# Six of eight quads in the seven-product form, with two weight sums of each made by accumulating transfers

## The chip, the cores and the metric

The kernel runs on one core of one Trainium2 chip. The metric is the time of one execution on the device in microseconds (us), given as the median of several runs.

## What is computed

A decoder trunk of two layers over 256 tokens of width 2048, in float32. Each layer adds a mixer (attention of two kinds in layer 0, latent attention in layer 1) and then a squared-ReLU MLP, which is where the change lies:

```python
def squared_relu_mlp(h, w_up, w_down):
    a = jnp.square(jax.nn.relu(h @ w_up))       # [256, 2048] @ [2048, 8192]
    return a @ w_down                           # [256, 8192] @ [8192, 2048]
x = x + squared_relu_mlp(rmsnorm(x, ln_mlp_g[layer]), w_up, w_down)
```

## The kernel before

**Number form.** A float32 matrix is handled as two rounded parts, hi (ScalarE, L707) and lo (VectorE, L1009: the value minus hi). A product is three matmuls (hi·hi, hi·lo, lo·hi) of 128x128 against 128x512 or 256 columns.

**Blocks.** The 8192 hidden columns are taken in four blocks (`b0`) per layer, so there are eight MLP blocks. A block has a stage "up" (32 weight pieces, which make the block's activations `a`, 16 tiles of 128), and a stage "down" over four column chunks of 512 of the output. Chunk 0 goes first (8 pieces, 32 to 39), chunks 1 and 2 go together as eight quads (pieces from 40 on, `quad_at(q)`), and chunk 3 goes last (8 pieces).

**Quads.** Quad q takes two k tiles (2q, 2q+1), both token halves and both column chunks: a 2 by 2 product of blocks. A plain quad makes the eight block products: two pieces and 24 matmuls. A fast quad makes seven (Winograd's variant of Strassen's form): 21 matmuls in pieces of 6, 6, 6 and 3, on the raw weights b11 and b21, the sums t0 and t1 ("t13"), the sums t2 and t3 ("t24"), and b22. It needs four sums of weights (`weight_sums`, VectorE, into `t_sum`, two buffers in turn) and four sums of token tiles (`token_sums` on VectorE, `token_sums_hi` on ScalarE L956, `token_sums_lo` on VectorE L1347). Before the change, quads 0, 1, 3, 5 and 7 are fast. Seven PSUM banks X1 to X7 hold the products and X8 the plain quads' last; after the quads ScalarE copies X1 and X8 to `c_sum` (L980), which frees the banks that chunk 3 uses, and VectorE's `combine` puts the products together in steps placed among the following pieces.

**Order of work.** Every engine has one queue in an order written out by hand. A weight is loaded by SyncE in 1 MB loads into four slots of `raw` (two pieces per load in the straight stages; in the quads two loads serve two quads) as soon as lo of the last piece of the load four before is done (`free_slot`). ScalarE makes hi of piece n once TensorE has used piece n-4 (four slots of `halves`), VectorE makes lo of it, TensorE uses it. In iteration j of the down loop, ScalarE and VectorE first split piece j+4 (`AHEAD`), and then do what the tables hang on that j: for VectorE

```python
sums = {35: 0, 37: 1, quad_at(2) - 3: 2, quad_at(4) - 3: 3, quad_at(6) - 3: 4}
```

so the weight sums of fast quad number m stand ahead of that quad's first splits. GpSimd makes constants, some products for the attention, and nothing in the MLP; no transfer is issued by it.

Of the kernel before, what the change touches and what calls it, by code (L numbers as in the profile page):

```python
# [31 lines left out]
P = 128  # L32
# [101 lines left out]
def all_pieces():  # L134
    out, seen = {}, set()

    def put(n, kind, load, half, count=0):
        out[n] = (kind, load, half, kind in ("raw", "b22") and load not in seen, count)
        if kind in ("raw", "b22"):
            seen.add(load)  # L140
    for n in range(P_MIX0, P_MLP0):
        put(n, "raw", n // 2, n % 2)
    for n in range(P_MIX1, P_MLP1):
        put(n, "raw", L_MIX1 + (n - P_MIX1) // 2, n % 2)
    for layer in range(2):
        for b0 in range(NB):
            for i, (kind, load, half) in enumerate(block_plan(layer, b0)):
                count = 15 * block_no(layer, b0) + 3 * load + (1 if kind == "t13" else 3) if kind[0] == "t" else 0
                put(block_base(layer, b0) + i, kind, load, half, count)
    return out  # L150
# [166 lines left out]
def build(nc, x, positions, ln_mix_g, ln_mlp_g, sf_w_in, sf_b_f, fox_q_g, fox_k_g, sf_w_o,  # L317
# [4 lines left out]
    with ExitStack() as ctx:  # L322
# [21 lines left out]
        with nc.sbuf_tensor("sd_last", [P, 4, 2, P], F32R) as sd_last:  # L344
# [63 lines left out]
        t_sum = [mix[:, 4096:6144].rearrange("p (i n) -> p i n", i=4),  # L408
                 heads_flat[:, 0:2048].rearrange("p (i n) -> p i n", i=4)]
        a_sum = heads_flat[:, 2048:2560].rearrange("p (i t) -> p i t", i=4)  # L410
        c_sum = mix[:, 6144:8192].rearrange("p (i n) -> p i n", i=4)

        def sd_of(i):
            return sd[:, i] if i < 4 else sd_last[:]

# [58 lines left out]
        rk_ready, k_scaled = sem("rk_ready"), sem("k_scaled")  # L474
        act_step, dve_step = sem("act_step"), sem("dve_step")
        t_step, a_step, sd_hi, sd_ready = sem("t_step"), sem("a_step"), sem("sd_hi"), sem("sd_ready")
        joint_copied, combined = sem("joint_copied"), sem("combined")
# [11 lines left out]
        def raw_piece(n):  # L489
# [5 lines left out]
            if kind[0] == "t":  # L495
                pair = 0 if kind == "t13" else 2
                return t_sum[load % 2][:, pair:pair + 2].rearrange("p i n -> p (i n)")
            piece = raw[:, load % SLOTS, half * size:(half + 1) * size]
# [108 lines left out]
        def _(pool):  # L607
# [74 lines left out]
            for n in (28, 29):  # L682
                split_out(n)


        @block.scalar
        def _(act):
# [8 lines left out]
            def split_hi(n):  # L696
# [257 lines left out]
            def token_sums_hi(no, i):  # L954
                act.wait_ge(a_step, 20 * no + 4 * i + 4)
# [39 lines left out]
        def _(dve):  # L995
# [317 lines left out]
            def weight_sums(layer, b0, m):  # L1313

                q = FAST_QUADS[m]
                one, two = pair_loads(layer, b0, q // 2)
                done = 15 * block_no(layer, b0) + 3 * m
# [3 lines left out]
                t = t_sum[m % 2]  # L1321
                b11_b12 = raw[:, one % SLOTS:two % SLOTS + 1:two % SLOTS - one % SLOTS, at:at + N]
                b12_b22 = raw[:, two % SLOTS, at:at + 2 * N].rearrange("p (i n) -> p i n", i=2)
                b21 = raw[:, one % SLOTS, at + N:at + 2 * N]
                v.tensor_tensor(t[:, 0:2], b12_b22, b11_b12, ALU.subtract).then_inc(t_step, 1)
                dve.wait_ge(t_step, done + 1)
                v.tensor_tensor(t[:, 2], b12_b22[:, 1], t[:, 0], ALU.subtract).then_inc(t_step, 1)
                dve.wait_ge(t_step, done + 2)
                v.tensor_tensor(t[:, 3], b21, t[:, 2], ALU.subtract).then_inc(t_step, 1)

            def token_sums(no, i):

                done = 20 * no + 4 * i
# [4 lines left out]
                v.tensor_tensor(a_sum[:, 0], y21, y22, ALU.add).then_inc(a_step, 1)  # L1338
                v.tensor_tensor(a_sum[:, 2], y11, y21, ALU.subtract).then_inc(a_step, 1)
                dve.wait_ge(a_step, done + 1)  # L1340
                v.tensor_tensor(a_sum[:, 1], a_sum[:, 0], y11, ALU.subtract).then_inc(a_step, 1)
                dve.wait_ge(a_step, done + 3)
                v.tensor_tensor(a_sum[:, 3], y12, a_sum[:, 1], ALU.subtract).then_inc(a_step, 1)

            def token_sums_lo(no, i):
                dve.wait_ge(sd_hi, 5 * no + i + 1)
                v.tensor_tensor(sd_of(i)[:, :, 1], a_sum, sd_of(i)[:, :, 0].bitcast(F32), ALU.subtract)                 .then_inc(sd_ready, 1)  # L1347
# [5 lines left out]
            def combine(no, step, base):  # L1353
# [5 lines left out]
                if step == 1:  # L1359
                    dve.wait_ge(joint_copied, 2 * no + 2)  # L1360
                    dve.wait_ge(pieces_used, base + quad_at(7) + 3)
                    v.tensor_tensor(p1_p6, X6, p1_p2, ALU.add).then_inc(combined, 1)
                elif step == 2:
# [11 lines left out]
                elif step == 7:  # L1375
                    after(5)
                    v.tensor_tensor(p1_p6_p7, X4, p1_p6_p7, ALU.add).then_inc(combined, 1)
                elif step == 8:
# [14 lines left out]
            def mlp_block(layer, b0):  # L1393
# [3 lines left out]
                for c in range(4):  # L1397
# [29 lines left out]
                for j in range(32, BLOCK_PIECES):  # L1427
# [36 lines left out]
        def _(pe):  # L1464
# [345 lines left out]
            def mlp_block(layer, b0):  # L1810
# [21 lines left out]
                for c in (0, 3):  # L1832
# [3 lines left out]
                    else:  # L1836
                        pe.wait_ge(cols_read, up0 + 4)
                        for q in range(8):
                            if q in FAST_QUADS:
                                pe.wait_ge(sd_ready, 5 * no + FAST_QUADS.index(q) + 1)  # L1840
                                fast_quad(base + quad_at(q), q, added0 + 1)
# [53 lines left out]
```

## Time and profile before

| | |
|---|---|
| median of 3 runs | 2073.39 us (2072.93 to 2074.01) |
| profiled execution | 2073.62 us, of which 2071.9 us from the first to the last instruction |
| TensorE / VectorE / ScalarE / GpSimd busy | 99% / 70% / 52% / 4% |
| memory traffic | 381.96 MB, 184 GB/s on average |
| one MLP block | 172.85 us (four in each layer) |
| eight quads of a block | 40.12 us |

The profile is of one execution. A busy TensorE is one with matmuls in its pipe, not one at its peak. The start-to-start distance of two matmuls, not the duration of one, says how fast it goes.

### The profile page before, as it was taken

The numbers are of one execution on the slowest core, as the hardware profiler recorded it, in microseconds if no ns is written. First come the engines' busy times: TensorE is split into PE (matmuls) and PEld (weight loads), VectorE is DVE, ScalarE is ACT, GpSimd is POOL, SyncE is SP. The second block draws the span as 40 slices with busy tenths as digits, with TensorE's granted clock in tenths as the row PEclk, the third lists the DMA queues.
The fourth block names the chain that finished last, engine by engine and source line by source line (L and its number), as shares of the span: only waits on it lengthen the run. The fifth ranks groups of instructions, "written<-read, shape, count | busy, mean of one in ns | idle before, by whom it ended". The sixth has DMA issues, their size and how long they took to land.

```text
span 2071.9 us, 25827 instructions
## 1 busy us (share of the span) xinstructions
PE 2060.6 (99%) x10360; PEld 1747.0 (84%) x10360; DVE 1453.8 (70%) x1904; ACT 1087.3 (52%) x1554; POOL 80.3 (4%) x120
## 2 busy tenths in 40 slices
PE   8999999999999999999999999999999999999999
PEld 7888888888888888888888898888888888888887
DVE  6545555567966876886797688557886696697787
ACT  6546565454544544554456676444554454454454
POOL 0000000000000000000000255000000000000000
PEclk9999999999999999999999999999999999999999
DMA  8544554555565565565555433465565665656554
GB/s 283 175 155 163 163 164 161 183 183 195 194 195 195 184 215 183 183 223 183 191 195 179 155 126 123 163 188 179 181 225 182 203 203 185 201 183 207 181 183 163
DMA packets 198479, 381.96 MB, mean 184 GB/s; under 512 B 10892, under 2 KB 17112, under 8 KB 198360
## 3 DMA queue, kind: packets, MB, share of 16 engines
q1 hardware_dynamic: 198312, 380.29, 56.4%
q8 instruction: 83, 1.36, 0.3%
q14 instruction: 36, 0.29, 0.0%
q10 hardware_dynamic: 48, 0.02, 0.0%
HBM read 378.19 MB, written 2.10 MB: 184 GB/s over the span
## 4 chain that ended last, share of the span: by engine, by line
PE 99%; POOL 0%; ACT 0%; DVE 0%; DMA 0%; issue 0%; SPq 0%; DVEq 0%; ACTq 0%
PE psum L1547 23%; PE psum L1478 14%; PE psum L1480 14%; PE psum L1479 14%; PE psum L1550 11%; PE psum L1778 5%; PE psum L1777 5%; PE psum L1776 5%; PE psum L1621 1%; PE psum L1704 1%; PE psum L1565 1%; PE psum L1681 0%; PE psum L1520 0%; PE psum L1665 0%; PE psum L1666 0%; PE psum L1705 0%
## 5 line engine op out<-in xcount | busy, mean ns | idle before, releaser
L1009 DVE TENSOR_TENSOR halves<-raw,halves 128x1024 fp32r<-128x1024 f32 (+1 forms) x724 | 854.7, 1189 | 456.4 <-ACT halves L707 451.3
L707 ACT CAST halves<-raw 128x1024 fp32r<-128x1024 f32 (+1 forms) x724 | 730.0, 1019 | 644.0 <-PE psum L1480 341.9
L1547 PE MATMUL psum<-h,halves 128*128 128x512 f32 x2048 | 639.0, 395 | 0.0
L1550 PEld LDWEIGHTS psum<-h,halves 128*128 128x128 f32 x2048 | 380.1, 188 | 87.7
L1550 PE MATMUL psum<-h,halves 128*128 128x256 f32 x2048 | 398.0, 278 | 0.0
L1478 PE MATMUL psum<-halves,a 128*128 128x512 f32 x828 | 325.5, 393 | 0.0
L1480 PE MATMUL psum<-halves,a 128*128 128x512 f32 x828 | 322.6, 390 | 0.0
L1479 PE MATMUL psum<-halves,a 128*128 128x512 f32 x828 | 322.3, 389 | 0.0
L1547 PEld LDWEIGHTS psum<-h,halves 128*128 128x128 f32 x2048 | 314.3, 189 | 2.8
L1478 PE MATMUL psum<-halves,h 128*128 128x512 f32 (+1 forms) x508 | 201.4, 397 | 0.0
L1480 PE MATMUL psum<-halves,h 128*128 128x512 f32 (+1 forms) x508 | 194.9, 384 | 0.0
L1479 PE MATMUL psum<-halves,h 128*128 128x512 f32 (+1 forms) x508 | 194.4, 383 | 0.0
L1480 PEld LDWEIGHTS psum<-halves,a 128*128 128x128 f32 x828 | 155.4, 188 | 32.8
L1478 PEld LDWEIGHTS psum<-halves,a 128*128 128x128 f32 x828 | 155.5, 188 | 31.8 <-ACT nat L774 0.4
L1479 PEld LDWEIGHTS psum<-halves,a 128*128 128x128 f32 x828 | 155.5, 188 | 31.5
L1776 PE MATMUL psum<-halves,a 128*128 128x512 f32 x312 | 121.4, 389 | 0.0
L1777 PE MATMUL psum<-halves,a 128*128 128x512 f32 x312 | 121.4, 389 | 0.0
L1778 PE MATMUL psum<-halves,a 128*128 128x512 f32 x312 | 121.4, 389 | 0.0
L1480 PEld LDWEIGHTS psum<-halves,h 128*128 128x128 f32 x508 | 95.3, 188 | 18.0
L1479 PEld LDWEIGHTS psum<-halves,h 128*128 128x128 f32 x508 | 95.6, 188 | 16.2
L1478 PEld LDWEIGHTS psum<-halves,h 128*128 128x128 f32 x508 | 95.6, 188 | 16.2
L707 ACT CAST halves<-mix 128x1024 fp32r<-128x1024 f32 x48 | 50.6, 1054 | 50.9 <-PE psum L1480 26.7
(251 smaller groups left out, 1861.5 us busy)
## 6 DMA issues: line engine op xcount, KB each, us to landing
raw<-in_mlp_w_up SPq DMA_DIRECT2D x128, 1024.0 KB, 5.3
raw<-in_mlp_w_down SPq DMA_DIRECT2D x128, 1024.0 KB, 5.2
raw<-in_sf_w_in SPq DMA_DIRECT2D x45, 1024.0 KB, 5.0
raw<-in_sf_w_o SPq DMA_DIRECT2D x16, 1024.0 KB, 5.1
raw<-in_mla_w_o SPq DMA_DIRECT2D x16, 1024.0 KB, 5.1
raw<-in_mla_w_down SPq DMA_DIRECT2D x8, 1024.0 KB, 5.1
raw<-in_mla_w_ukv SPq DMA_DIRECT2D x8, 1024.0 KB, 5.5
raw<-in_mla_w_uq SPq DMA_DIRECT2D x8, 768.0 KB, 4.6
```

The lines of the kernel that those rows point to most:

```text
L707: nc.scalar.copy(half_piece(n, 0), raw_piece(n)).then_inc(hi_done, 1)
L1009: v.tensor_tensor(half_piece(n, 1), raw_piece(n), half_piece(n, 0).bitcast(F32), ALU.subtract)\
L1478: mm(bank, x_hi, hi[:, i], start=(k == 0), stop=False)
L1479: mm(bank, x_hi, lo[:, i], start=False, stop=False)
L1480: last = mm(bank, x_lo, hi[:, i], start=False, stop=(k == total_kts - 1))
L1547: last = mm(bank, half_piece(n, 0)[:, cols], src[:, k].rearrange("p s t -> p (s t)"), start=(k == 0), stop=(k == KT - 1))
L1550: last = mm(bank[:, T:2 * T], half_piece(n, 1)[:, cols], src[:, k, 0], start=False, stop=False)
L1565: ins = nc.tensor.transpose(psum[:, bank + i // 2, col:col + P], x_tok[:, tt, k * P:(k + 1) * P], ident[:])
L1621: ins = nc.tensor.transpose(TURN[:, i * P:(i + 1) * P], s, ident[:])
L1776: mm(bank, x_hi, w_hi, start=start, stop=False)
L1777: mm(bank, x_hi, w_lo, start=False, stop=False)
L1778: return mm(bank, x_lo, w_hi, start=False, stop=stop)
```

## The change

One more quad is fast: quads 0, 1, 3, 4, 6 and 7 (plain: 2 and 5), so a block has 76 pieces in place of 74. The signs of the sums are chosen anew, so that t0 = b11 + b12 and t1 = b22 + b12: GpSimd loads b11 and b22 into `t_sum` and, when both have landed, issues two transfers that add b12 from memory onto them. VectorE makes only t2 = b11 + t1 and t3 = b21 + t2. `t_sum` has a third buffer, which is the space of `c_sum`; so the copies of X1 and X8 both wait until the last quad's t24 is split. Token sums of the sixth fast quad are made among chunk 0's pieces and kept in `sd_nat`, in the space of `s_buf`.

```diff
-FAST_QUADS = 0, 1, 3, 5, 7
-PLAIN_QUADS = 2, 4, 6
+FAST_QUADS = 0, 1, 3, 4, 6, 7
+PLAIN_QUADS = 2, 5
...
-                 heads_flat[:, 0:2048].rearrange("p (i n) -> p i n", i=4)]
+                 heads_flat[:, 0:2048].rearrange("p (i n) -> p i n", i=4),
+                 mix[:, 6144:8192].rearrange("p (i n) -> p i n", i=4)]
...
+            def neighbour_sums(layer):
+
+                w = mlp_w_down[layer]
+                for b0 in range(NB):
+                    base, no = block_base(layer, b0), block_no(layer, b0)
+                    for m, q in enumerate(FAST_QUADS):
+                        fast_no = len(FAST_QUADS) * no + m + 1
+                        if m >= 3:
+                            pool.wait_ge(lo_done, base + quad_at(FAST_QUADS[m - 3]) + 3)
+                        elif b0 == 0:
+                            pool.wait_ge(lo_done, base + 8)
+                        else:
+                            pool.wait_ge(lo_done, base - BLOCK_PIECES + quad_at(FAST_QUADS[m + 3]) + 3)
+                            if m == 2:
+                                pool.wait_ge(x_added, (ADDED_MLP0, ADDED_MLP1)[layer] + 4 * (b0 - 1) + 3)
+                        t = t_sum[m % 3]
+                        rows = [slice(b0 * D + (2 * q + k) * P, b0 * D + (2 * q + k + 1) * P) for k in range(2)]
+                        b11, b12, b22 = w[rows[0], N:2 * N], w[rows[0], 2 * N:3 * N], w[rows[1], 2 * N:3 * N]
+                        pool.dma_start(t[:, 0], b11).then_inc(t_loaded, 16)
+                        pool.dma_start(t[:, 1], b22).then_inc(t_loaded, 16)
+                        pool.wait_ge(t_loaded, 32 * fast_no)
+                        pool.dma_start(t[:, 0], b12, accum_op=ALU.add).then_inc(t_summed, 16)
+                        pool.dma_start(t[:, 1], b12, accum_op=ALU.add).then_inc(t_summed, 16)
+
+            neighbour_sums(0)
             pool.wait_ge(rope_ready, 1)
...
             for n in (28, 29):
                 split_out(n)
+            neighbour_sums(1)
...
-                    act.wait_ge(t_step, count)
+                    act.wait_ge(t_summed if kind == "t13" else t_step, count)
...
-                    for at, slot, bank in ((quad_at(7) - 1, 3, X8), (quad_at(7), 0, X1)):
-                        if j == at:
-                            act.wait_ge(pieces_used, base + at + 1)
-                            nc.scalar.copy(c_sum[:, slot], bank).then_inc(joint_copied, 1)
+                    if j == 34:
+                        token_sums_hi(no, 5)
+                    if j == quad_at(7):
+                        act.wait_ge(pieces_used, base + quad_at(7) + 1)
+                        act.wait_ge(lo_done, base + quad_at(7) + 3)
+                        nc.scalar.copy(c_sum[:, 0], X1).then_inc(joint_copied, 1)
+                        nc.scalar.copy(c_sum[:, 3], X8).then_inc(joint_copied, 1)
...
-                for load in (one, two):
-                    dve.wait_ge(raw_loaded[load % SLOTS], 16 * (load // SLOTS + 1))
+                dve.wait_ge(raw_loaded[one % SLOTS], 16 * (one // SLOTS + 1))
+                dve.wait_ge(t_summed, 32 * fast_no)
...
-                v.tensor_tensor(t[:, 0:2], b12_b22, b11_b12, ALU.subtract).then_inc(t_step, 1)
-                dve.wait_ge(t_step, done + 1)
-                v.tensor_tensor(t[:, 2], b12_b22[:, 1], t[:, 0], ALU.subtract).then_inc(t_step, 1)
-                dve.wait_ge(t_step, done + 2)
-                v.tensor_tensor(t[:, 3], b21, t[:, 2], ALU.subtract).then_inc(t_step, 1)
+                t = t_sum[m % 3]
+                b11, b21 = (raw[:, one % SLOTS, at + k * N:at + (k + 1) * N] for k in range(2))
+                v.tensor_tensor(t[:, 2], b11, t[:, 1], ALU.add).then_inc(t_step, 1)
+                dve.wait_ge(t_step, 2 * fast_no - 1)
+                v.tensor_tensor(t[:, 3], b21, t[:, 2], ALU.add).then_inc(t_step, 1)
...
-                sums = {35: 0, 37: 1, quad_at(2) - 3: 2, quad_at(4) - 3: 3, quad_at(6) - 3: 4}
+                sums = {34: 0, 37: 1, quad_at(2) - 3: 2, quad_at(3) - 1: 3, quad_at(5) - 2: 4, quad_at(6) - 1: 5}
...
                     if j == 33:
                         token_sums_lo(no, 4)
+                        token_sums(no, 5)
+                    if j == 35:
+                        token_sums_lo(no, 5)
```

Left out of the diff: the counts of semaphores, the signs in `token_sums` and two `combine` steps that go with the new signs, and the declarations.

## Rows read from the trace of the kernel before

**Rows 1.** The page: busy time of each engine, clock, and the chain that ended last.

```profile
PE 2060.6 (99%) x10360; PEld 1747.0 (84%) x10360; DVE 1453.8 (70%) x1904; ACT 1087.3 (52%) x1554; POOL 80.3 (4%) x120
...
PEclk9999999999999999999999999999999999999999
...
PE 99%; POOL 0%; ACT 0%; DVE 0%; DMA 0%; issue 0%; SPq 0%; DVEq 0%; ACTq 0%
```

**Rows 2.** Waits of TensorE: engine, line, releaser, total us, times, longest.

```profile
PE psum L1557 <- DMA nat<-in_ln_mix_g: 4.0, 1, 4.0
PE psum L1579 <- DMA x_tok<-in_x: 1.3, 2, 1.0
PE psum L1621 <- DVE mix L1181: 1.2, 1, 1.2
PE psum L1621 <- POOL mix L677: 1.1, 1, 1.1
```

**Rows 3.** Windows: one block, its quads, chunk 3 (clock, DMA share, GB/s last).

```profile
584.35:757.20 172.85, 172.85 (x882) 147.13 (x881) 129.50 (x142) 86.00 (x89) 0.00 (x0) 1.00 0.60 195
...
695.35:735.47 40.12, 40.12 (x179) 33.22 (x178) 35.65 (x37) 25.37 (x28) 0.00 (x0) 1.00 0.52 170
735.47:757.20 21.73, 21.73 (x97) 18.02 (x96) 18.79 (x22) 8.95 (x9) 0.00 (x0) 1.00 0.85 286
```

**Rows 4.** VectorE's groups by shape: count, busy us, mean ns, idle before.

```profile
L1009 DVE TENSOR_TENSOR halves<-raw,halves 128x1024 fp32r<-128x1024 f32 x664 | 811.0, 1230 | 446.7 <-ACT halves L707 441.8
...
L1325 DVE TENSOR_TENSOR mix<-raw 128x1024 f32<-128x1024 f32 x24 | 29.3, 1219 | 0.0
L1009 DVE TENSOR_TENSOR halves<-raw,halves 128x512 fp32r<-128x512 f32 x42 | 28.7, 684 | 2.8 <-ACT halves L707 2.8
...
L1329 DVE TENSOR_TENSOR mix<-raw,mix 128x512 f32<-128x512 f32 x24 | 16.6, 692 | 0.8
...
L1338 DVE TENSOR_TENSOR heads<-nat 128x128 f32<-128x128 f32 x40 | 11.4, 285 | 0.0
```

**Rows 5.** Timeline of VectorE about quads 0, 1 and 3.

```profile
692.39 1.22 DVE L1325 TENSOR_TENSOR heads<-raw 128x1024 f32<-128x1024 f32 x1
...
694.98 1.22 DVE L1009 TENSOR_TENSOR halves<-mix,halves 128x1024 fp32r<-128x1024 f32 x1
...
699.69 2.36 DVE L1009 TENSOR_TENSOR halves<-heads,halves 128x1024 fp32r<-128x1024 f32 x2 [0.44 <-ACT halves L707]
...
709.03 2.35 DVE L1009 TENSOR_TENSOR halves<-mix,halves 128x1024 fp32r<-128x1024 f32 x2
```

**Rows 6.** Timeline of ScalarE: a split ahead of quad 4, and quad 7's copies.

```profile
692.88 1.05 ACT L707 CAST halves<-mix 128x1024 fp32r<-128x1024 f32 x1 [1.67 <-PE psum L1480]
...
711.92 1.05 ACT L707 CAST halves<-raw 128x1024 fp32r<-128x1024 f32 x1 [0.79 <-PE psum L1778]
...
732.32 1.05 ACT L707 CAST halves<-raw 128x1024 fp32r<-128x1024 f32 x1 [0.31 <-PE psum L1778]
733.27 0.58 ACT L980 COPY mix<-psum 128x512 f32<-128x512 f32 x1
```

**Rows 7.** DMA issues of the page: count, KB each, median us from issue to landing.

```profile
raw<-in_mla_w_uq SPq DMA_DIRECT2D x8, 768.0 KB, 4.6
```

**Rows 8.** SyncE's loads of MLP weights by line: issue in ns, and landings.

```profile
L562 SPq DMA_DIRECT2D raw<-in_mlp_w_down x128: 367/368/507, 475.4 to 2043.4; - x128
...
DMA to landing us min/median/max: 5.0/5.2/8.9
```

**Rows 9.** Timeline of SyncE: the load that quads 4 and 5 use.

```profile
699.27 0.37 SPq L562 DMA_DIRECT2D raw<-in_mlp_w_down  x1
```

**Rows 10.** Window in the start, when the DMA engines are full.

```profile
10.00:15.00 5.00, 5.00 (x25) 4.11 (x24) 3.82 (x5) 2.83 (x4) 0.00 (x0) 1.00 1.06 379
```

**Rows 11.** Timeline of GpSimd and VectorE side by side in layer 1's mixer.

```profile
1198.15 1.75 POOL L661 TENSOR_TENSOR mix<-mix,st 128x512 f32<-128x512 f32 x1 [7.72 <-DVE st L1176]
...
1198.92 2.06 DVE L1009 TENSOR_TENSOR halves<-raw,halves 128x1024 fp32r<-128x1024 f32 x1
```

More of the change, by code:

```diff
@@ L147, in all_pieces @@
             for i, (kind, load, half) in enumerate(block_plan(layer, b0)):
-                count = 15 * block_no(layer, b0) + 3 * load + (1 if kind == "t13" else 3) if kind[0] == "t" else 0
+                fast_no = len(FAST_QUADS) * block_no(layer, b0) + load + 1
+                count = {"t13": 32 * fast_no, "t24": 2 * fast_no}.get(kind, 0)
                 put(block_base(layer, b0) + i, kind, load, half, count)
@@ L334, in build @@
         halves = sb("halves", [P, SLOTS, 2, 2 * N], F32R)
+        with nc.sbuf_tensor("sd_nat", [P, 4, 2, P], F32R) as sd_nat:
+            pass
         nat = sb("nat", [P, 2, TT, N])
@@ L413, in sd_of @@
         def sd_of(i):
-            return sd[:, i] if i < 4 else sd_last[:]
+            return sd[:, i] if i < 4 else (sd_last, sd_nat)[i - 4][:]
         def out_on_pool(n):
@@ L475, in build @@
         act_step, dve_step = sem("act_step"), sem("dve_step")
+        t_loaded, t_summed = sem("t_loaded"), sem("t_summed")
         t_step, a_step, sd_hi, sd_ready = sem("t_step"), sem("a_step"), sem("sd_hi"), sem("sd_ready")
@@ L496, in raw_piece @@
                 pair = 0 if kind == "t13" else 2
-                return t_sum[load % 2][:, pair:pair + 2].rearrange("p i n -> p (i n)")
+                return t_sum[load % 3][:, pair:pair + 2].rearrange("p i n -> p (i n)")
             piece = raw[:, load % SLOTS, half * size:(half + 1) * size]
@@ L954, in token_sums_hi @@
             def token_sums_hi(no, i):
-                act.wait_ge(a_step, 20 * no + 4 * i + 4)
+                act.wait_ge(a_step, 24 * no + 4 * i + 4)
                 nc.scalar.copy(sd_of(i)[:, :, 0], a_sum).then_inc(sd_hi, 1)
@@ L1315, in weight_sums @@
                 q = FAST_QUADS[m]
-                one, two = pair_loads(layer, b0, q // 2)
-                done = 15 * block_no(layer, b0) + 3 * m
-                for load in (one, two):
-                    dve.wait_ge(raw_loaded[load % SLOTS], 16 * (load // SLOTS + 1))
+                one, _ = pair_loads(layer, b0, q // 2)
+                fast_no = len(FAST_QUADS) * block_no(layer, b0) + m + 1
+                dve.wait_ge(raw_loaded[one % SLOTS], 16 * (one // SLOTS + 1))
+                dve.wait_ge(t_summed, 32 * fast_no)
                 at = q % 2 * 2 * N
[L1321 to L1324, printed above, removed]
-                v.tensor_tensor(t[:, 0:2], b12_b22, b11_b12, ALU.subtract).then_inc(t_step, 1)
-                dve.wait_ge(t_step, done + 1)
-                v.tensor_tensor(t[:, 2], b12_b22[:, 1], t[:, 0], ALU.subtract).then_inc(t_step, 1)
-                dve.wait_ge(t_step, done + 2)
-                v.tensor_tensor(t[:, 3], b21, t[:, 2], ALU.subtract).then_inc(t_step, 1)
+                t = t_sum[m % 3]
[3 more added lines that the diff above has]
+                v.tensor_tensor(t[:, 3], b21, t[:, 2], ALU.add).then_inc(t_step, 1)
             def token_sums(no, i):
-                done = 20 * no + 4 * i
+                done = 24 * no + 4 * i
                 if done:
@@ L1337, in token_sums @@
                 y11, y21, y12, y22 = (y_buf[:, k0 + k, tt * P:(tt + 1) * P] for k in range(2) for tt in range(TT))
-                v.tensor_tensor(a_sum[:, 0], y21, y22, ALU.add).then_inc(a_step, 1)
-                v.tensor_tensor(a_sum[:, 2], y11, y21, ALU.subtract).then_inc(a_step, 1)
+                v.tensor_tensor(a_sum[:, 0], y21, y22, ALU.subtract).then_inc(a_step, 1)
+                v.tensor_tensor(a_sum[:, 2], y21, y11, ALU.subtract).then_inc(a_step, 1)
                 dve.wait_ge(a_step, done + 1)
-                v.tensor_tensor(a_sum[:, 1], a_sum[:, 0], y11, ALU.subtract).then_inc(a_step, 1)
+                v.tensor_tensor(a_sum[:, 1], y11, a_sum[:, 0], ALU.subtract).then_inc(a_step, 1)
                 dve.wait_ge(a_step, done + 3)
@@ L1345, in token_sums_lo @@
             def token_sums_lo(no, i):
-                dve.wait_ge(sd_hi, 5 * no + i + 1)
+                dve.wait_ge(sd_hi, 6 * no + i + 1)
                 v.tensor_tensor(sd_of(i)[:, :, 1], a_sum, sd_of(i)[:, :, 0].bitcast(F32), ALU.subtract)                 .then_inc(sd_ready, 1)
@@ L1361, in combine @@
                     dve.wait_ge(pieces_used, base + quad_at(7) + 3)
-                    v.tensor_tensor(p1_p6, X6, p1_p2, ALU.add).then_inc(combined, 1)
+                    v.tensor_tensor(p1_p6, X6, p1_p2, ALU.subtract).then_inc(combined, 1)
                 elif step == 2:
@@ L1376, in combine @@
                     after(5)
-                    v.tensor_tensor(p1_p6_p7, X4, p1_p6_p7, ALU.add).then_inc(combined, 1)
+                    v.tensor_tensor(p1_p6_p7, X4, p1_p6_p7, ALU.subtract).then_inc(combined, 1)
                 elif step == 8:
@@ L1839, in mlp_block @@
                             if q in FAST_QUADS:
-                                pe.wait_ge(sd_ready, 5 * no + FAST_QUADS.index(q) + 1)
+                                pe.wait_ge(sd_ready, 6 * no + FAST_QUADS.index(q) + 1)
                                 fast_quad(base + quad_at(q), q, added0 + 1)
```

## The prediction

> **What bounds the kernel now.** I read the page first. TensorE is busy 99% of the span and the chain that ended last is 99% TensorE at the full granted clock [rows 1]; the reader is to see that no other engine has a share there. The view of waits then says whether TensorE ever stands still in the MLP: its four waits are together 7.6 us, all in the start or in a mixer (L1557, L1579, L1621), none in an MLP block [rows 2]. So a matmul less in a block is time won, if nothing new makes TensorE wait, and a gain from shorter waits can't exist there: there are none. The windows give the rate: a block takes 172.85 us, its quads 40.12 us [rows 3]. By the code the quads are 5 x 21 + 3 x 24 = 177 matmuls (the window counts 179, with those in flight at its edges), so one starts every 40.12 / 177 = 0.2267 us.
>
> VectorE is busy 35.65 of those 40.12 us and 129.50 of the block's 172.85, ScalarE 25.37 and 86.00, GpSimd nothing [rows 3]. VectorE's slack in the quads is thus 4.5 us, and what happens there decides.
>
> **TensorE's part.** Quad 4 becomes fast (fast quads 5 and 7 move to 6 and 7, plain ones 4 and 6 to 5): 24 - 21 = 3 matmuls less per block, 24 in all, 24 x 0.2267 = 5.44 us. A fast quad lasts 21 x 0.2267 = 4.76 us, a plain one 5.44 us, and the quads together 39.44 us.
>
> **VectorE's part.** Per block the three sums of five quads go: 5 x (1.22 + 0.69 + 0.69) = 13.0 us [rows 4]. Two sums of six quads come: 6 x 1.38 = 8.3 us. One fast quad more splits three pieces of 1024 and one of 512 instead of two of 1024: 3 x 1.23 + 0.68 - 2 x 1.23 = +1.9 us. A sixth set of token sums is four instructions of 0.285 us and a split of 0.69: at most +1.8 us, in chunk 0, where a piece lasts 12 x 0.2267 = 2.72 us and a split 1.23. Net -1.0 us per block. In the quads' own window: 35.65 - 3 x 2.60 + 4 x 1.38 + 1.9 = 35.3 of 39.4 us, as full as before (0.89). The densest stretch, two fast quads in a row, now comes three times instead of once; each needs 2 x 4.37 us of splits and about 1.4 of sums, 10.1 us against 9.5 of TensorE, and a plain quad (2.5 against 5.4 us) or the straight pieces give it back. The pair 0, 1 of before had a like load (1.4 us of x sums in its midst) and made no wait [rows 2]. I cost this at 0; without that cover it is 0.6 us for each of three pairs, 14 us in all.
>
> **ScalarE's part.** +1.7 us of splits and +0.6 for the token sums, of a block in which it is idle half the time: 0. Its copies of X1 and X8 now stand together behind the split of chunk 3's first piece. Before, that split began at 732.32 and the second copy ended at 733.85, with the quads' end at 735.47 [rows 3, 6]. With one copy of 0.58 us more, the end comes at about 734.4 on that clock, and 1.0 us are left until TensorE asks for both (`joint_copied`). The new wait for the last t24's lo holds nothing up as long as TensorE itself, which uses that piece 2.72 us into quad 7, isn't late. Cost 0; if the cover went, what exceeds 1.0 us counts eight times. Behind the waiting copy stands chunk 3's second piece, which has 2.7 us more.
>
> **The transfers.** 48 quads x 4 = 192 transfers of 256 KB, 50 MB on top of 382. TensorE doesn't read them; the quad's t13 split on ScalarE and the two sums on VectorE wait for them (`t_summed`), and behind VectorE's wait stand the splits of the quad itself. For fast quads number 0 to 2 of a block the buffer is free a whole "up" stage ahead (some 80 us), so they are hidden. For numbers 3, 4, 5 (quads 4, 6, 7) the loads may go only when the t24 of the quad three before is split, and GpSimd does them strictly in turn.
>
> The budget: number 3 may start when VectorE has split piece 42. Before, that ended at 696.2; with sums 1.2 us shorter ahead of it, ScalarE's hi (until 693.93) leads and it ends at about 695.1 [rows 5, 6]. TensorE comes to quad 4 at 695.35 + 3 x 4.76 + 5.44 = 715.1; lo of its first piece (1.23) and the sums (1.38) must go before, so the transfers must be down by 712.4: 17.3 us. Number 5 may start once piece 52 is split, 711.4 at the latest [rows 5]; quad 7 starts at 695.35 + 5 x 4.76 + 2 x 5.44 = 730.0, so it is needed by 727.4: 16.0 us. If L is one chain (two loads, wait, two adding transfers) and p what of it holds GpSimd's queue, the three in turn need 695.1 + 2p + L <= 727.4, so 2p + L <= 32.3 us.
>
> The price of a chain: no transfer by GpSimd and no adding one is in the trace. By the nearest rows, 1 MB lands in 5.2 us and 768 KB in 4.6 [rows 7, 8], 0.6 us per 256 KB and a fixed part of 2.8: one 256 KB load 3.4 us. An issue costs SyncE 0.37 us [rows 8]; GpSimd's longest instruction took 1.75 us [rows 11]. I take 1 us (nearer the issue row, doubled and more for software's sake). An adding transfer reads twice: +1.2 us for the pair. So L = 2 + 3.4 + 2 + 3.4 + 1.2 = 12.0 us and p = 7.4 us; 2p + L = 26.8. With 1 us more in each half for SyncE's loads beside it, L = 14 and 2p + L = 30.8: both still fit. Lower end: issues of 0.37, no double read: L = 8.3. Upper end: issues of 1.75 and landings slowed in each half by the 3.7 us between median and longest [rows 8]: L = 22.4, p = 14.1, 2p + L = 50.6, 18.3 us too late in each block, 146 us.
>
> The Trainium skill (DMA: Bandwidth & Descriptors, Anatomy of one DMA) gives 2.0 us plus bytes / 436e3 for such a transfer; an estimate by that page would be about 2.6 us each, L near 10 and so an easier fit. No run here shows it yet.
>
> Have the DMA engines room? Full, they move 379 GB/s [rows 10]. The quads had 170 GB/s, chunk 3 286 [rows 3]. Some four chains fall in the quads: 4.2 MB, 6.3 with double reads, in 39.4 us, +107 to +160 GB/s: 277 to 330, below 379. SyncE's loads have slack: that of quads 4 and 5 was issued at 699.27, landed some 5.2 us later and was first read at 711.92, 7 us after [rows 6, 8, 9]. Cost 0; bound: the same 3.7 us, still covered.
>
> **The sum.** 2073.62 (the profiled execution: span 2071.9 and 1.7 around it) - 5.44 = 2068.18; the median lies 0.23 lower, so **2067.95 us**.
>
> **The rivals.**
> *The chain is too slow* (ends on the other side). Place: VectorE's wait for `t_summed` ahead of quads 4, 6, 7. It decides from 2p + L = 32.3 us on, that is L = 14.8 with what is added to my 12.0 split evenly over the two halves; each further us of L then costs 2 us a block, 16 us in all. With L = 17, 2p + L = 36.8, 4.5 us too late, 36 us in all: 2104. For it: the double read and the issue are unpriced, and my own value with load leaves 1.5 us of that sum. Against it: traffic has room, and the median landing is near the shortest. Chance 0.20.
>
> *GpSimd's descriptor work slows VectorE.* Beside a GpSimd instruction one lo split took 2.06 instead of 1.23 us [rows 11]. If each issue did so, 16 issues in the quads would add 16 x 0.83 = 13.3 us to 35.3, 9 us over TensorE's 39.4; some 2 us of it the splits made ahead can cover, so 7 x 8 = 56 us, 2124. Against it: that GpSimd instruction reads two tensors, an issue none. The Trainium skill (SBUF — State Buffer, SBUF: two separate sides) has a rule for this: a VectorE instruction with two SBUF inputs and a GpSimd instruction exclude each other only if the latter reads SBUF, while a VectorE instruction in two-port mode keeps GpSimd from writing descriptors. By it the case falls away here, since the MLP's VectorE work is nearly all two-input float32; the 2.06 us row agrees with its first half. Chance 0.05.
>
> *Small waits eat the gain:* a late copy or split in the dense pairs, 0.2 to 0.6 us a block, 1.6 to 4.8 us: about 2070.5. For it: slacks of 1 us and less. Against: none showed before at like slacks. Chance 0.10.
>
> The remaining 0.65 is the forecast.
>
> **Range and chances.** A run of this kernel tells 0.2% (4.1 us) from no change. The forecast's own range is 2067.2 to 2069.2. Below it nothing is to be had. Upwards I go through the small waits and into the slow chain where it costs up to 2 us a block more than the gain: 2084. Faster 0.65, same 0.09, slower 0.26 (both slow rivals and a little of the small waits).
>
> **What would show it.** Quads of 39.4 us, block 172.2; 10336 matmuls; no TensorE wait in a block. On VectorE L1325 gone, idle time ahead of the sums none. In GpSimd's transfers a landing under 5 us for loads and under 7 for adding ones. Wrong would be: VectorE or ScalarE idle until a transfer lands, lo splits above 1.3 us in the MLP, or SyncE's loads beyond 9 us.

## The result and the profile after

| | before | after |
|---|---|---|
| median of 5 runs each | 2074.01 us (2072.93 to 2074.12) | 2117.08 us (2114.63 to 2118.23) |
| profiled execution, its span | 2073.62, 2071.9 us | 2114.63, 2112.9 us |
| mean granted clock | 1.000 | 0.992 |

The ratio after to before is 1.0206, with a 95% interval of 1.0195 to 1.0217: slower by 43 us. The forecast was 2067.95 us, the range ended at 2084; the rival "the chain is too slow" gave 2104 at L = 17, and the time is 13 us above that.

The page after: the engines' busy times (against [rows 1]), the chain that ended last by engine and by line, and the issues of the new transfers.

```profile
PE 2071.6 (98%) x10336; PEld 1753.3 (83%) x10336; DVE 1445.7 (68%) x1936; ACT 1102.0 (52%) x1578; POOL 220.8 (10%) x312
...
PE 84%; DMA 10%; DVE 2%; POOL 1%; issue 1%; ACT 1%; SPq 0%; DVEq 0%; ACTq 0%
PE psum L1580 23%; PE psum L1511 14%; PE psum L1513 14%; PE psum L1512 14%; PE psum L1583 11%; DMA mix<-in_mlp_w_down 6%; DMA heads<-in_mlp_w_down 3%; PE psum L1809 1%; PE psum L1811 1%; DVE halves L1043 1%; PE psum L1810 1%; PE psum L1654 1%; PE psum L1737 1%; PE psum L1598 0%; ACT halves L738 0%
...
mix<-in_mlp_w_down POOLq DMA_DIRECT2D x128, 256.0 KB, 6.9
...
heads<-in_mlp_w_down POOLq DMA_DIRECT2D x64, 256.0 KB, 7.4
```

The matmuls fell by 24 as meant, and VectorE lost 8.1 us. But the chain that ended last, 99% TensorE before [rows 1], is now 10% transfers. That the chain names `mix` (6%) and `heads` (3%), the homes of `t_sum`, says which transfers. The view of waits tells who stood still (engine, tile, line, releaser: us in total, times, longest):

```profile
POOL mix L667 <- DMA mix<-in_mlp_w_down: 179.3, 32, 8.8
...
POOL heads L667 <- DMA heads<-in_mlp_w_down: 119.6, 16, 8.7
...
DVE mix L1357 <- DMA mix<-in_mlp_w_down: 35.4, 8, 4.8
...
PE psum L1809 <- DVE halves L1043: 30.4, 8, 4.2
```

L667 is the first adding transfer, which waits for the two loads; L1357 is t2 of `weight_sums`, L1809 a matmul of a fast quad. GpSimd's own 299 us cost nothing by themselves. TensorE waits eight times, once in each block, 30.4 us in all, where it had no wait in an MLP block before [rows 2].

Which quad? GpSimd's timeline in the block whose quads begin at 700.69 (start, us, line, tile, and in brackets its idle time and what ended it). L664 and L665 are the loads of b11 and b22, L667 and L668 the adding ones:

```profile
700.86 0.57 POOL L664 DMA_DIRECT2D mix<-in_mlp_w_down  x1 [108.09 <-DVE halves L1043]
...
705.21 0.90 POOL L667 DMA_DIRECT2D mix<-in_mlp_w_down  x1 [3.23 <-DMA mix<-in_mlp_w_down]
...
707.63 0.57 POOL L664 DMA_DIRECT2D heads<-in_mlp_w_down  x1 [0.61 <-DVE halves L1043]
...
717.48 0.90 POOL L667 DMA_DIRECT2D heads<-in_mlp_w_down  x1 [8.73 <-DMA heads<-in_mlp_w_down]
...
718.59 1.25 POOL L664 DMA_DIRECT2D mix<-in_mlp_w_down  x1
...
729.21 0.90 POOL L667 DMA_DIRECT2D mix<-in_mlp_w_down  x1 [8.81 <-DMA mix<-in_mlp_w_down]
729.77 1.25 POOL L668 DMA_DIRECT2D mix<-in_mlp_w_down  x1
```

Number 3's loads were waited for 3.2 us, those of numbers 4 and 5 8.7 and 8.8. From number 4 GpSimd goes straight on to number 5 (718.59 has no bracket), so the lateness is handed on. The last adding transfer, issued at 729.77, is what everything waits for. The chain of waits through that stretch (start, us, what held the end):

```profile
729.77 6.74 DMA mix<-in_mlp_w_down
...
736.60 0.70 DVE mix L1357
...
738.02 1.15 DVE halves L1043
...
739.30 0.47 PE psum L1809
```

And TensorE's timeline at the same place:

```profile
735.14 0.39 PE L1811 MATMUL psum<-halves,sd_last 128*128 128x512 f32 x1
739.30 0.47 PE L1809 MATMUL psum<-halves,a 128*128 128x512 f32 x1 [3.77 <-DVE halves L1043]
...
740.55 0.63 PE L1810 MATMUL psum<-halves,a 128*128 128x512 f32 x1
740.98 0.63 PE L1811 MATMUL psum<-halves,a 128*128 128x512 f32 x1
...
743.49 0.39 PE L1811 MATMUL psum<-halves,sd_nat 128*128 128x512 f32 x1
743.72 0.39 PE L1809 MATMUL psum<-halves,sd_nat 128*128 128x512 f32 x1
```

The reader is to see two losses. Quad 7 begins 3.9 us late (739.30 instead of 735.37). And behind the wait a matmul starts every 0.43 us (740.55, 740.98) until 743.49, then every 0.23 again. The windows of quads 0 to 6, of the slow stretch and of what follows show it in the granted clock, the third number from the end:

```profile
700.62:735.37 34.75, 34.75 (x155) 28.57 (x153) 27.64 (x29) 20.74 (x22) 9.89 (x14) 1.00 0.93 277
739.30:743.50 4.20, 4.20 (x12) 3.28 (x13) 3.45 (x4) 2.12 (x4) 1.69 (x3) 0.59 0.83 123
743.50:745.78 2.28, 2.28 (x11) 1.87 (x10) 1.28 (x2) 1.70 (x3) 0.00 (x0) 1.00 0.97 344
```

For 4.2 us the grant is 0.59 on the mean, most of it the half level (1.2 of 2.4 GHz). From 739.30 to 743.49 are eleven distances, 4.19 us where 11 x 0.2267 = 2.49 would do: 1.7 us lost besides the wait.

The span rose by 41.0 us, over 24 matmuls fewer: 41.0 + 5.4 = 46.4 us of loss, of which 30.4 are the waits. The 16.0 left, 2.0 a block, are the slow matmuls behind each wait (1.6 to 1.7 us in six blocks, 2.6 and 2.8 in two) and, in every block, 0.2 between the wait (3.77 us in the block shown) and the distance less a matmul's (4.16 - 0.23).

### The profile page after: what moved, and what is told of

Its sections match the earlier page's. It is cut to its first block, busy times and chain, and to the rows that moved or that the text cites. A ratio compares the mean times of both kernels' runs of the same rounds, so it can differ in the third digit from the quotient of the medians.

```text
span 2112.9 us, 26073 instructions
## 1 busy us (share of the span) xinstructions
PE 2071.6 (98%) x10336; PEld 1753.3 (83%) x10336; DVE 1445.7 (68%) x1936; ACT 1102.0 (52%) x1578; POOL 220.8 (10%) x312
## 4 chain that ended last, share of the span: by engine, by line
PE 84%; DMA 10%; DVE 2%; POOL 1%; issue 1%; ACT 1%; SPq 0%; DVEq 0%; ACTq 0%
PE psum L1580 23%; PE psum L1511 14%; PE psum L1513 14%; PE psum L1512 14%; PE psum L1583 11%; DMA mix<-in_mlp_w_down 6%; DMA heads<-in_mlp_w_down 3%; PE psum L1809 1%; PE psum L1811 1%; DVE halves L1043 1%; PE psum L1810 1%; PE psum L1654 1%; PE psum L1737 1%; PE psum L1598 0%; ACT halves L738 0%
## 5 line engine op out<-in xcount | busy, mean ns | idle before, releaser
L1511 PE MATMUL psum<-halves,a 128*128 128x512 f32 x828 | 325.8, 393 | 0.0
L1513 PE MATMUL psum<-halves,a 128*128 128x512 f32 x828 | 322.9, 390 | 0.0
L1512 PE MATMUL psum<-halves,a 128*128 128x512 f32 x828 | 322.5, 390 | 0.0
L664 POOL DMA_DIRECT2D mix<-in_mlp_w_down x32 | 29.5, 921 | 1067.4 <-DVE halves L1043 877.0
L1809 PE MATMUL psum<-halves,a 128*128 128x512 f32 x272 | 109.2, 401 | 30.4 <-DVE halves L1043 30.4
L1513 PEld LDWEIGHTS psum<-halves,h 128*128 128x128 f32 x508 | 95.4, 188 | 17.9
L1811 PE MATMUL psum<-halves,a 128*128 128x512 f32 x272 | 109.4, 402 | 0.0
L1810 PE MATMUL psum<-halves,a 128*128 128x512 f32 x272 | 108.7, 400 | 0.0
```

The lines of the kernel that those rows point to most:

```text
L664: pool.dma_start(t[:, 0], b11).then_inc(t_loaded, 16)
L1511: mm(bank, x_hi, hi[:, i], start=(k == 0), stop=False)
L1512: mm(bank, x_hi, lo[:, i], start=False, stop=False)
L1513: last = mm(bank, x_lo, hi[:, i], start=False, stop=(k == total_kts - 1))
L1809: mm(bank, x_hi, w_hi, start=start, stop=False)
L1810: mm(bank, x_hi, w_lo, start=False, stop=False)
```

## The experiments

Line numbers shift by a few between kernels; the tiles and the releaser tell the same places. The "budget" below is the prediction's: number 3's first load to the landing of number 5's last transfer may take 32.3 us. In the eight blocks of the changed kernel it took 35.2 to 36.0. Medians over the blocks, from the start of an issue to the landing, in us:

| kernel | 3 to 4 | 4 to 5 | whole chain 3 | 4 | 5 | sum to the end of 5 |
|---|---|---|---|---|---|---|
| predicted (budget 32.3) | 8.4 | 8.4 | 14 | 14 | 14 | 30.8 |
| changed kernel | 6.8 | 10.6 | 13.5 | 18.4 | 17.9 | 35.6 |
| plain_b12 | 6.8 | 9.7 | 12.2 | 16.6 | 17.5 | 34.5 |
| half_weights | 6.8 | 9.0 | 11.6 | 15.4 | 19.0 | 34.9 |
| half_through_chunk3 | 6.8 | 9.0 | 11.6 | 15.7 | 17.0 | 33.1 |
| half_and_plain | 6.8 | 8.2 | 10.3 | 13.3 | 12.5 | 27.7 |

### Is it the adding? (plain_b12)

```diff
-                        pool.dma_start(t[:, 0], b12, accum_op=ALU.add).then_inc(t_summed, 16)
-                        pool.dma_start(t[:, 1], b12, accum_op=ALU.add).then_inc(t_summed, 16)
+                        pool.dma_start(t[:, 0], b12).then_inc(t_summed, 16)
+                        pool.dma_start(t[:, 1], b12).then_inc(t_summed, 16)
```

> The two adding transfers of each fast quad overwrite with b12 instead of adding it (so t0 and t1 are b12, part of the sums is left out). All 192 transfers, waits and bytes moved from memory stay. Theory A (the adding itself is slow, 6.3 and 8.4 us to landing, and the next quad's loads stand behind it in GpSimd's one queue): the second pair lands in about 4 us like a lone pair of loads, the three chains have a period near 6 us, quad 7 is in time, no wait of TensorE, clock 1.0, 2068 us (2067 to 2070). Theory B (SyncE's weight loads beside them slow all of GpSimd's transfers): landings stay at 6 to 9 us, and the time at 2105 to 2118.

Measured: 2097.76 us (2096.78 to 2100.2), ratio 1.0115 (1.010 to 1.013), clock 0.996. TensorE still waits in each block, and VectorE for a transfer:

```profile
DVE mix L1357 <- DMA mix<-in_mlp_w_down: 24.3, 8, 3.9
...
PE psum L1809 <- DVE halves L1043: 19.4, 8, 3.2
```

That the transfers add costs 2117.1 - 2097.8 = 19 us of the loss of 43. The rest stays with transfers that only load, so the adding is one cause and not the only one; the time lies in neither of the two ranges that I had named. The edit takes away more than the sum itself: the issues are shorter too (0.54 us in place of 0.90 and 1.25), and the packets are of 4 KB in place of 2.

### Is it the order on GpSimd? (loads_on_sp)

SyncE issues b11 and b22 among its own loads, GpSimd only the adding ones; each buffer has its own semaphores.

```diff
+                        if (l, i) == (2, 0):
+                            neighbours(b0, 3, base + quad_at(0) + 3)
+                        if (l, i) == (2, 1):
+                            neighbours(b0, 4, base + quad_at(1) + 3)
+                        if (l, i) == (3, 1):
+                            neighbours(b0, 5, base + quad_at(3) + 3)
...
-                        pool.dma_start(t[:, 0], b11).then_inc(t_loaded, 16)
-                        pool.dma_start(t[:, 1], b22).then_inc(t_loaded, 16)
```

> The loads of b11 and b22 are issued by SyncE, at the same readiness, between its weight loads; only the adding transfers stay on GpSimd's queue. Theory A (order in GpSimd's queue): the loads land in 3 to 6 us whatever is being added, the adding ones stay at 6 to 8.5 us, quad 7's chain is down about 13 us after piece 52 is split, 3 us in time: 2068 us (2067 to 2071). Theory B (bandwidth shared with SyncE's weight loads): the loads still take 8 to 10 us and the wait ahead of quad 7 stays: 2095 to 2118.

Measured: 2087.63 us (2086.36 to 2089.09), ratio 1.0065 (1.005 to 1.008), clock 0.999. The waits, and the issues with their median landings:

```profile
PE psum L1824 <- DVE halves L1058: 13.4, 8, 2.6
```

```profile
mix<-in_mlp_w_down SPq DMA_DIRECT2D x64, 256.0 KB, 4.9
...
mix<-in_mlp_w_down POOLq DMA_DIRECT2D x64, 256.0 KB, 8.0
```

With the loads off GpSimd's queue, TensorE's wait falls from 30.4 to 13.4 us but stays: number 5's loads no longer wait for number 4's to land, yet the adding transfers land no sooner (8.0 us), and SyncE's small loads take 4.9 us in `mix` and 7.2 in `heads`, not 3.3. So the strict turn accounts for a part, and a part is in the transfers themselves. This time too lies between my two ranges.

### Only the last quad off the transfers (last_on_vector, last_early)

Quad 7's t0 and t1 are VectorE's again (two sums of 0.69 us); the other five fast quads stay with the transfers. In last_on_vector they stand right before t2; in last_early one piece sooner.

```diff
+ON_VECTOR = 5,
...
+                if m in ON_VECTOR and part == 0:
+                    v.tensor_tensor(t[:, 0], b11, b12, ALU.add).then_inc(v_summed, 1)
+                    v.tensor_tensor(t[:, 1], b22, b12, ALU.add).then_inc(v_summed, 1)
+                    return
...
+                    if j == quad_at(6) - 2:
+                        weight_sums(layer, b0, 5, 0)
```

> Quad 7's t0 and t1 are made by VectorE (two more sums of 512 columns, 1.38 us a block), the other five quads stay as they are. If the one wait ahead of quad 7 and the half clock behind it are the whole loss of 46 us, both go: 2068 us (2067 to 2070), clock 1.0. Rival: quads 4 and 6 are late as well, or the 1.38 us make VectorE late in the pair 6, 7: waits of 0.5 us or more a block remain, 2072 to 2085.

Measured: last_on_vector 2076.36 us (2075.42 to 2077.11), ratio 1.0011 (1.0001 to 1.002), clock 1.000: the forecast of 2068 missed, the rival's range (2072 to 2085) right. Of the engines that compute only ScalarE waits for GpSimd's transfers there, five times by at most 1.1 us. TensorE keeps a small wait:

```profile
PE psum L1831 <- DVE halves L1055: 5.0, 8, 0.6
```

VectorE's timeline in last_on_vector says why: idle first, then four sums, and the split that TensorE wants only behind them.

```profile
726.00 0.69 DVE L1055 TENSOR_TENSOR halves<-raw,halves 128x512 fp32r<-128x512 f32 x1 [0.78 <-ACT halves L750]
726.61 0.69 DVE L1374 TENSOR_TENSOR mix<-raw 128x512 f32<-128x512 f32 x1
727.21 0.69 DVE L1375 TENSOR_TENSOR mix<-raw 128x512 f32<-128x512 f32 x1
727.93 0.69 DVE L1379 TENSOR_TENSOR mix<-raw,mix 128x512 f32<-128x512 f32 x1
728.66 0.69 DVE L1381 TENSOR_TENSOR mix<-raw,mix 128x512 f32<-128x512 f32 x1
729.27 1.22 DVE L1055 TENSOR_TENSOR halves<-raw,halves 128x1024 fp32r<-128x1024 f32 x1
```

So two of the sums were moved into the idle 0.78 us ahead:

> As the run with quad 7's t0 and t1 on VectorE, but those two sums stand one piece sooner in its queue (behind the split of quad 6's t24, where it stood idle 0.8 us) and not right ahead of quad 7's first split. If the 0.8 us of wait a block left in that run is only this place in VectorE's order, it goes: 2068.5 us (2067.5 to 2070). Rival: the 1.38 us are too much for the pair 6, 7 wherever they stand, and the wait stays at 0.5 us or more: 2073 to 2077.

Measured: last_early **2068.46 us** (2067.86 to 2069.2), ratio 0.9975 (0.9965 to 0.9984), clock 1.000: 5.3 us under the kernel before, and the fastest of all that were run. Its page:

```profile
PE 2055.9 (99%) x10336; PEld 1742.8 (84%) x10336; DVE 1453.2 (70%) x1952; ACT 1100.8 (53%) x1578; POOL 197.3 (10%) x280
```

TensorE has no wait in any MLP block, with all 10336 matmuls and the sixth fast quad. TensorE's term of the prediction (5.44 us) holds, and with it the zeros for token sums, dense pairs and late copies. The loss sits in the transfers of quad 7 alone. Number 4's whole chain still takes 18.4 us here, but sums done 25.2 us after number 3's start are in time.

### No transfers at all (all_on_vector)

All six quads have their four sums on VectorE (`ON_VECTOR = 0, 1, 2, 3, 4, 5`, and otherwise as in last_on_vector).

> No transfers by GpSimd: VectorE makes all four sums of all six quads. By my count of VectorE it has 35.3 + 4 x 1.38 = 40.8 us of work in quads of 39.4 us. Theory VectorE-full: 1 to 1.5 us of waits a block, 2076 to 2090 with what the clock adds. Rival, the splits made ahead take it up: 2068 us, and then the transfers are not needed at all.

Measured: 2098.92 us (2097.91 to 2099.88), ratio 1.0119 (1.0103 to 1.0136), clock 1.000: the right theory, but above its range (2076 to 2090), which had 1 to 1.5 us of waits in a block. TensorE waits three times in a block:

```profile
PE psum L1831 <- DVE halves L1055: 14.7, 16, 1.1
...
PE psum L1831 <- DVE x_tok L1403: 8.6, 8, 1.1
```

Six fast quads without transfers would thus cost 25 us: the transfers are worth having where they are in time. Waits of 1 us, even three in a block, left the granted clock at 1.000. They aren't quite free beside their own length, though: each costs 0.16 us more up to the first matmul and 0.1 in the matmuls behind it, 6 us over the 24.

### Five fast quads, sums by transfers (five_transfers)

```diff
-FAST_QUADS = 0, 1, 3, 4, 6, 7
-PLAIN_QUADS = 2, 5
+FAST_QUADS = 0, 1, 3, 5, 7
+PLAIN_QUADS = 2, 4, 6
```

> Quads 0, 1, 3, 5, 7 as in the kernel before, with the changed kernel's sums by transfers, three buffers and late copies: the transfers alone, without the sixth quad. A plain quad stands between the chains of numbers 3 and 4, and the last chain needs only the second buffer: no wait, 2074 us as before (within 2). Rival: the transfers cost something by themselves (later weight loads, slower VectorE): above 2078.

Measured: 2074.31 us (2073.16 to 2075.35), ratio 1.0003 (0.9993 to 1.0012), clock 1.000, with no TensorE wait in a block. 160 of the 192 transfers, half of them adding, and both late copies cost nothing that can be measured. It needs two chains behind the start of the quads, not three: number 3's start to the end of number 4 takes 24.7 us.

### SyncE's loads made smaller (half_weights, half_through_chunk3, half_and_plain)

SyncE's 1 MB loads compete for the same DMA engines. In half_weights those of the quads bring only half of each row; in half_through_chunk3 chunk 3's too; half_and_plain adds plain_b12 to that.

```diff
-                        down(load, of[load], l)
+                        free_slot(load)
+                        half = raw[:, load % SLOTS].rearrange("p (k n) -> p k n", k=4)[:, :, 0:N // 2]
+                        src = w_down[b0 * D + 4 * P * l:b0 * D + 4 * P * (l + 1), of[load] * N:of[load] * N + N // 2]
+                        sp_.dma_start(half, src.rearrange("(k p) n -> p k n", p=P)).then_inc(raw_loaded[load % SLOTS], 16)
```

> Of the changed kernel, with SyncE's eight loads for the quads of a block bringing the first 256 of each 512 columns (the other halves keep what stood there, so part of the weights is left out); all instructions of the engines and GpSimd's 192 transfers stay. Theory B (in the quads the two queues take turns on the same DMA engines, and a chain waits out SyncE's 1 MB loads): landings of GpSimd's first loads of quads 6 and 7 fall from 7 to 10 us to 4 to 6, the three chains end 8 us sooner, no wait ahead of quad 7, 2068 us (2067 to 2071). Theory A (only what GpSimd itself has queued): they stay at 7 to 9 us, behind its own adding transfers, and the time stays above 2095.

Measured: 2104.4 us (2101.91 to 2108.85), ratio 1.015 (1.0137 to 1.0164), clock 0.994: only 13 us regained. The time lies in theory A's range (above 2095), but the next run doesn't bear that theory out. By the table the first two chains are quicker (4 to 5 in 9.0 us), but number 5 takes 19.0 us, longer than before the edit. It falls where SyncE loads chunk 3, and those loads were still whole.

> As the run with half the columns in SyncE's loads for the quads, and chunk 3's four loads halved as well (part of the weights left out), because two whole loads of chunk 3 were in flight under quad 7's adding transfers there. If what was left of the wait (3 us a block) came from those two, quad 7's adding transfers land in 5 to 7 us instead of 9, and the time falls to 2068 to 2085. If it is GpSimd's own queue that is left, the wait ahead of quad 7 stays at 2 us or more a block: 2085 to 2105.

Measured: 2081.83 us (2077.62 to 2083.61), ratio 1.0035 (1.0023 to 1.0047), clock 0.999, within the range named for chunk 3's loads (2068 to 2085), with a rest of the wait:

```profile
PE psum L1816 <- DVE halves L1050: 9.6, 7, 2.4
```

> The same, and the adding transfers overwrite instead (sums left out too): both suspected prices are taken away at once. Theory 'two causes' (adding at half rate ahead of the next loads, and SyncE's loads between): the three chains have a period under 8 us, no wait ahead of quad 7: 2068 us (2067 to 2070). If a wait of 1 us or more a block stays, there is a third cause: software issue or the fixed part of four landings in a row, above 2075.

Measured: 2069.63 us (2068.77 to 2070.61), ratio 0.9981 (0.9972 to 0.999), clock 1.000, all three chains by 27.7 us and one wait of TensorE in the MLP blocks:

```profile
PE psum L1816 <- DVE halves L1050: 1.1, 1, 1.1
```

The two causes together account for the loss: halving SyncE's loads through chunk 3 gives 35 us back, not adding another 12. They don't simply add up (not adding gave 19 by itself), since only what exceeds the budget costs anything.

### Another quad off the transfers (quad6_on_vector)

`ON_VECTOR = 4,`: quad 6's t0 and t1 on VectorE, quad 7's back with the transfers. GpSimd then has only one chain ahead of quad 7's.

> Only quad 6's t0 and t1 are made by VectorE; quads 4 and 7 keep the transfers. The chain of quad 7 then starts with an empty GpSimd queue when piece 52 is split. My theory (a lone chain takes 13 to 15 us, as number 3's does; the loss came from three chains in a row with a period of 11 us): it lands about 725 on the changed kernel's clock, 2 us in time, no wait, 2068.5 us (2067.5 to 2071). Rival (quad 7 is late whatever stands ahead of it): a wait of 2 to 4 us a block stays, 2090 to 2117.

Measured: 2076.18 us (2071.91 to 2080.21), ratio 1.0009 (1.0 to 1.0019), clock 0.999. I missed here, and the rival's range (2090 to 2117) didn't hold either: VectorE waits for quad 7's sums in six of eight blocks.

```profile
DVE mix L1379 <- DMA mix<-in_mlp_w_down: 6.7, 6, 3.3
...
PE psum L1831 <- DVE halves L1055: 5.7, 6, 3.2
```

GpSimd's queue was free when quad 7's turn came, at 710.39. Its loads were still waited for 6.0 us and its whole chain took 17.3 us as the median (13.0 to 19.2), where number 3's took 13.4:

```profile
710.39 0.57 POOL L676 DMA_DIRECT2D mix<-in_mlp_w_down  x1 [8.68 <-DVE halves L1055]
...
717.52 0.90 POOL L679 DMA_DIRECT2D mix<-in_mlp_w_down  x1 [6.01 <-DMA mix<-in_mlp_w_down]
```

So a chain is slow at this place without another chain ahead of it; only SyncE's loads lie beside it. Ending 32.3 us after number 3's start as the median, it stands right at the budget of 32.3, and the wide spread of the times (8 us) goes with that.

## Why the prediction was wrong

**The step that failed** is "2p + L = 30.8: both still fit". It used one p and one L for all three chains. For number 3, whose loads find the DMA engines idle, they were nearly right: L was to be 12 to 14 us and is 13.0 to 14.6, p 7.4 to 8.4 and is 6.8. But number 4's queue time is 10.6, and number 5's L 17.9: 6.8 + 10.6 + 17.9 = 35.3 (35.6 as the median of the sums), 3.3 over the budget of 32.3. With 0.3 us from the split of piece 42 to the first issue and 0.1 from the last landing to VectorE's start, that is the 3.8 us of TensorE's wait as the mean of the blocks. The budget itself, 32.3 us, was right: on the clock of after it runs from 700.55 to 735.37 - 2.6 = 732.8, 32.2 us. Built on it, the rival "the chain is too slow" named the place, VectorE's wait for `t_summed`; of its three quads only quad 7 made TensorE wait.

**Why the chains stretch.** I let the sum of bytes decide: 277 to 330 GB/s are below 379, so there is room, and 1 us for each half is enough. The mean was right (277 GB/s in the window of quads 0 to 6) and decided nothing: in that window the DMA engines' share is 0.93, not the three quarters that 277 of 379 would be. The windows within it show how uneven the load is; the first and third lie in adding transfers, the second in SyncE's loads:

```profile
709.00:712.00 3.00, 3.00 (x15) 2.48 (x14) 2.84 (x5) 2.48 (x3) 0.00 (x0) 1.00 1.07 209
715.00:720.00 5.00, 5.00 (x24) 4.14 (x23) 3.90 (x6) 2.75 (x4) 2.52 (x4) 1.00 1.05 377
722.00:725.00 3.00, 3.00 (x15) 2.49 (x14) 2.71 (x4) 2.34 (x3) 0.00 (x0) 1.00 1.08 208
```

The engines are full in all three, but move 208 GB/s where they add and 377 where they load. I had charged the double read of the adding as 1.2 us a pair by bytes; number 3's pair lands 6.7 and 8.2 us after issue, its pair of plain loads 3.3 and 3.5. And a transfer issued while the engines are full waits its turn: number 4's loads, issued right behind number 3's adding ones, landed after 7.3 and 9.0 us. The experiments bear both out, each with its size, in half_and_plain and its two parts.

The packet records show the turns themselves. On idle engines an adding pair's first packet starts 1.6 us after the issue (number 0 in six blocks). For numbers 3, 4 and 5 it starts 4.0, 4.0 and 3.3 us after it (medians), and in the time between, SyncE's packets fill the engines. The block shown, from 705 to 709 and from 709 to 712 (q1 is SyncE's queue, q0 GpSimd's; packets, MB, share of the engines): number 3's adding pair is issued at 705.21 and 705.77, and up to 709 only SyncE's load moves.

```profile
q1 hardware_dynamic: 418, 0.85, 80.8%
...
q0 software_dynamic: 226, 0.43, 86.0%
q1 hardware_dynamic: 111, 0.20, 20.7%
```

So two terms of the chain can be set against their measures. SyncE's loads hold up the three adding pairs by 2.4 + 2.4 + 1.7 = 6.5 us a block, where I had put 1 us in each half, 4 us in the whole sum. The double read was sized nearly right: the 256 packets of a pair at 178 ns fill the 16 engines for 2.8 us, GpSimd's 128 plain ones of 4 KB at 159 ns for 1.3, so +1.6 us against my +1.2. What no run divides is the wait of the plain loads: number 3's first packet starts 1.3 us after its issue, number 5's 6.4, behind number 4's adding pair and SyncE's loads together.

**SyncE's loads** I costed at nothing with up to 3.7 us more. The bound was too small and the zero right for TensorE. In the stretch of 705 to 720 us they were the slow ones too:

```profile
raw<-in_mlp_w_down SPq DMA_DIRECT2D x3, 1024.0 KB, 11.2
mix<-in_mlp_w_down POOLq DMA_DIRECT2D x4, 256.0 KB, 8.0
heads<-in_mlp_w_down POOLq DMA_DIRECT2D x4, 256.0 KB, 7.9
```

Over all blocks their landings went from 5.0/5.2/8.9 us [rows 8] to 5.0/5.5/11.9, past the 9 us that I had named as a sign. ScalarE waited for them three times, 5.4 us in all; TensorE never did.

**The missing term.** The rival's price counted only the wait, 16 us for each us of L: at the 3.8 us measured it gives 30 us, and TensorE's waits are 30.4. The 16 us of slow matmuls behind them were in no case, and they put the time 13 us above the rival's 2104 although its wait (4.5 us) was longer than the one measured.

**TensorE's part**: -5.44 us predicted, -5.3 measured in last_early as a whole; 10336 matmuls. Right.

**VectorE's part**: -1.0 us a block predicted, 1453.8 - 1445.7 = 8.1 us in eight blocks measured. Right. The dense pairs cost nothing in last_early and five_transfers.

**ScalarE's part**: +2.3 us a block predicted, 1102.0 - 1087.3 = 14.7 in eight, 1.8, measured. The copies of X1 and X8 ran at 742.65 and 743.13, 0.58 us each, and chunk 3's first matmul started at 745.78 without a wait. Right; their slack was larger here because quad 7 itself was late, and last_early shows that it suffices without that.

**GpSimd slows VectorE**: refuted. VectorE's splits of 128x1024 take 1228 ns on the mean, against 1230 before [rows 4], with 192 issues beside them:

```profile
L1043 DVE TENSOR_TENSOR halves<-raw,halves 128x1024 fp32r<-128x1024 f32 x656 | 800.9, 1228 | 443.5 <-ACT halves L738 439.8
```

By the Trainium skill (SBUF — State Buffer, SBUF: two separate sides) a VectorE instruction with two SBUF inputs is held up only by GpSimd work that reads SBUF; the trace agrees with these 1228 ns.

**The estimate by the page on transfers.** The Trainium skill (DMA: Bandwidth & Descriptors, Anatomy of one DMA) gave some 2.6 us for each 256 KB, an estimate, and L near 10. The first load of a lone chain landed after 3.1 to 3.3 us and the second adding one at a median of 8.4: the measurement decides, and that estimate was further off than the bound from the rows.

**Small waits eat the gain**: seen only in last_on_vector, where 0.6 us a block, 5.0 in all, and 2.3 beside these waits took back the gain. The wait is of that rival's size, the 2.3 were in no case of mine, and it came from sums on VectorE that the change doesn't have.

**Chances.** The rival's terms for it, "the double read and the issue are unpriced, and my own value with load leaves 1.5 us", were the ones that carried. A 0.65 for a case whose margin was 1.5 us of 32.3, with a range for L of 8.3 to 22.4, was too much.

## What to carry to other kernels

When transfers run in a strict chain, price each by what shares the DMA engines in its own stretch, not one price for all and not a mean rate against a peak: here the first chain took 13.5 us and the third 17.9. Price the second loss behind a wait of TensorE too: those of some 4 us cost another 2 us each, while waits of about 1 us cost only 0.3 more. Where only the last link of a chain is late, take that link alone off it and leave the rest: that turned a loss of 43 us into a gain of 5.3.

## What the runs showed of the hardware

- An adding transfer from memory holds the DMA engines about twice as long as a load of the same bytes: 208 GB/s at a share of 1.07 to 1.08 against 377 at 1.05. In the packet records a 2 KB packet that adds took 178 ns, a plain one of 2 KB on SyncE's queue 84 ns, and a plain one of 4 KB on GpSimd's queue 159 ns.
- GpSimd's issue of an adding transfer takes 0.90 us and the next 1.25, that of a plain load 0.57 (1.25 when adding ones stand ahead of it), but the second of a pair starts 0.56 us after the first in either case. In plain_b12 all issues took 0.54.
- The clock's half level didn't follow every wait of TensorE. Taken from the start of one matmul to the start of the next, over all runs but without the start of the program, it came behind none of the 74 of 0.9 to 2.3 us (24 of them 1.15 to 1.47 us in all_on_vector), behind six of the nine of 2.7 to 3.2 us, and behind all 16 of 3.5 to 4.6 us. What decided among the nine the runs don't settle.
- Two queues slowed each other by whole transfers (for 4 us only SyncE's packets moved while an issued adding pair stood, 705 to 709): SyncE's 1 MB loads took 11.2 us as the median from 705 to 720 us, 5.2 before [rows 8], while loads of 256 KB on GpSimd's queue took 7 to 9 instead of 3.3.
